# TensorE leaves out the products without use in the passages between stages

## The chip, the cores and the metric

The kernel runs on one core of one Trainium2 chip. The metric is the device time of one execution in microseconds (us). It is one program for a two-part transformer stack over 256 tokens of width 1024: an attention, RWKV and mixture-of-experts layer, followed by two layers of another block. Only passages of these two last layers are touched.

## The reference, cut to what matters

```python
def second_block(x, ...):
    for l in range(DEPTH_2):                      # DEPTH_2 = 2
        h = rms_norm_2(x, norm_mix_pre[l])
        proj = h @ w_in[l]                        # 1024 x 3072: 12 slices of 256
        ...                                       # convolution, two attentions, gated convolution
        mix = jnp.concatenate([y_conf, y_sb, y_ret, y_sc], axis=-1) @ w_out[l]
        x = x + rms_norm_2(mix, norm_mix_post[l])
        f = conv_ffn(rms_norm_2(x, norm_ffn_pre[l]), ffn_up[l], ffn_conv_w[l], ffn_down[l])
        x = x + rms_norm_2(f, norm_ffn_post[l])
    return x
```

Everything is float32. `rms_norm_2` divides each token by the root of its mean square and multiplies by a gain. Each layer has two places where a norm stands between two large products: x into the mixer (`w_in`) and x into the feed-forward part (`ffn_up`). A norm needs the whole row of a token, so the product ahead of it must be complete before the product behind it can start.

## The kernel before, in words

The kernel first runs the first block (front part, recurrence, experts) and then `layers_part` (L2628). Each engine there has one function with a fixed order of work: `layers_tensor` (TensorE, PE in the profile), `layers_scalar` (ACT), `layers_vector` (DVE), `layers_sync` (SP, which starts the loads). They meet in semaphores alone. `signalled` (L2708) waits for a count of a named signal, `free` (L2790) waits until a bank of PSUM has been read by its last user.

The stream x is kept with tokens on the partitions (`m.x_tok`), in two tiles t of 128 tokens. A product wants the channels on the partitions. `turn` (L2796) does the turning and the scaling by the norm in one step: for each tile t and each of the eight chunks c of 128 channels, one float32 product of the chunk with `scale_eye`, a 128x128 diagonal matrix of 1/root. It is called four times in all: `turn("turn_mix", 0)` at the head of each layer and `turn("turn_ffn", 2)` between mixer and feed-forward part of each layer. These are the four passages.

What runs in a passage, in the order of dependence:

- The last product before it (`tokens_product`, L2904, or the expert part's L2103) fills four banks: two halves of tile 0, then two halves of tile 1.
- ACT squares and sums each bank (L3044) and takes a root (L3049). DVE multiplies by the gain (L3182), scales and adds to x (L3188 or L3194).
- ACT squares the new x (L3020, or L3028 and L3032) and takes the second root (L3022 or L3036). DVE makes the reciprocal (L3169) and the diagonal (L3171), and signals "scaled" for this tile.
- TensorE waits for "scaled" (L2807) and turns the tile (L2810). ACT copies the banks to `x_hi` with the gain (L3061 or L3135), in a rounded format. DVE makes `x_lo`, what the rounding left (L3239 or L3366).
- The product behind the passage (`entry_product`, L2842) starts on the first chunk as soon as it is there. Weights are split likewise into `w_hi` (ACT, L3010) and `w_lo` (DVE, L3216), and each float32 product is made of three of the rounded format. After it come the long runs of `product` (L2868).

Between the last product before the passage and the turned tile, TensorE has nothing to do. In the kernel before, `turn` issues products there whose result nobody reads: a matrix of ones times a table, 512 columns wide, in float32, into a bank that is overwritten next. At `turn_mix` they stand ahead of tile 0 (L2801, two in the first layer and three in the second). At `turn_ffn` they stand between tile 0 and tile 1 (L2806, three in each layer), behind one more wait for a free bank.

Of the kernel before, what the change touches and what calls it, by code (L numbers as in the profile page):

```python
# [2627 lines left out]
def layers_part(nc, m, a, out, ctx):  # L2628
# [66 lines left out]
    def before(l, unit):  # L2695
        b, n = unit
        return l * USES[b] + n
# [10 lines left out]
    def signalled(eng, l, name, k):  # L2708
        eng.wait_ge(S[name], l * total[name] + k)
# [78 lines left out]
    def layers_tensor(pe):  # L2788
        for l in range(2):
            def free(name, k=0):  # L2790
                unit = UNIT[name, k]
                if before(l, unit) > 0:
                    pe.wait_ge(drained[unit[0]], before(l, unit))
                return unit[0]

            def turn(name, first):  # L2796

                banks = [free(name, n) for n in range(4)]

                for _ in range(0 if first > 0 else 3 if l > 0 else 2):  # L2800
                    pe.matmul(m.ps[:, banks[0], :], m.c("ones"), m.c("iota"), start=True, stop=True)  # L2801
                for t in range(TT):
                    if t > 0 and first > 0:
                        b = free("up_first")
                        for _ in range(3):
                            pe.matmul(m.ps[:, b, :], m.c("ones"), m.c("iota"), start=True, stop=True)  # L2806
                    signalled(pe, l, "scaled", first + t + 1)  # L2807
                    for c in range(KC):
                        cols = slice(c % 2 * SEQ + t * P, c % 2 * SEQ + (t + 1) * P)
                        mm = pe.matmul(m.ps[:, banks[c // 2], cols], m.x_tok[:, t, c * P:(c + 1) * P],  # L2810
                                       scale_eye[:, t, :], start=True, stop=True)
                        if t == TT - 1 and c % 2:
                            mm.then_inc(filled[banks[c // 2]], 1)
# [80 lines left out]
            def tokens_product(i, banks, x, chunk, first, last, tiles=range(TT)):  # L2894
# [15 lines left out]
                return mm  # L2910

            turn("turn_mix", 0)
            project("conf_a")
            project("conf_gate")
# [3 lines left out]
            b = free("vec")  # L2918
# [7 lines left out]
            for i, name in enumerate(("ret_q", "ret_k")):  # L2926
                await_drained(pe, l, name)
                b = free("swap", i)
# [3 lines left out]
            for h in range(4):  # L2932
                signalled(pe, l, "sb_masked", h + 1)
                b = free("tail", h)
# [16 lines left out]
            b = free("ret_mean")  # L2951
# [3 lines left out]
            b = free("ret_var")  # L2955
            pe.matmul(m.ps[:, b, :], m.c("pair_ones"), ret_sq[:, :, :], start=True, stop=True).then_inc(filled[b], 1)
            signalled(pe, l, "conf_done", 1)
            b = free("conf_mean")
# [4 lines left out]
            banks = [free("out", n) for n in range(4)]  # L2963
            for r, t in ((0, None), (1, None), (2, 0), (3, 0), (2, 1), (3, 1)):
# [6 lines left out]
                if r == 0:  # L2971
                    signalled(pe, l, "conf_squared", 1)
                    b = free("conf_var")
                    for c in range(2):
                        mm = pe.matmul(m.ps[:, b, 0:SEQ], m.c("ones"), conf_sq[:, c, :], start=(c == 0), stop=(c == 1))
                    mm.then_inc(filled[b], 1)
            turn("turn_ffn", 2)
            for q, (kind, n) in enumerate(FFN_ORDER):
                i = PIECE_FFN + q
# [6 lines left out]
                if n == 0:  # L2986
                    banks = [free("down", k) for k in range(4)]
# [526 lines left out]
```

## Time and profile before

| | |
|---|---|
| median of 3 runs | 1357.8 us (1356.83 to 1359.24) |
| the profiled execution's own time | 1356.83 us |
| its span, first to last instruction | 1355.0 us |
| PE busy | 1160.0 us (86%) |
| DVE busy | 737.7 us (54%) |
| ACT busy | 487.1 us (36%) |
| DMA queue q1 | 347.40 MB, 70.6% of 16 engines' time |
| mean granted TensorE clock | 0.939 |

The layers' part begins near 733 us. The four passages lie near 734, 850, 1042 and 1158 us. Before it, from some 320 to 730 us, the expert weights are loaded and the DMA engines are busy throughout; the granted clock of TensorE changes there between 1.00 (2.4 GHz) and 0.50 (1.2 GHz). In the rows below, a float32 product shows as two records of PE MATMUL and two of PEld LDWEIGHTS, and a row of a timeline merges neighbouring records of one line. The number in square brackets at the end is how long the engine had been idle before, and what released it. A row of the windows gives a stretch, its length, the busy time and instruction count of PE, PEld, DVE, ACT and POOL, then TensorE's granted clock, the share of the DMA engines and GB/s.

### The profile page before, as it was taken

How to read it: one execution, taken by the hardware profiler on the slowest of the kernel's cores; microseconds unless marked ns; L12 is line 12 of the kernel's file. 1: busy time of each engine (PE TensorE's matmuls, PEld its weight loads, DVE VectorE, ACT ScalarE, POOL GpSimd, SP SyncE). 2: the span in 40 equal slices, each digit the busy share in tenths (PEclk: the TensorE clock that was granted, in tenths of full speed). 3: DMA queues.
4: the chain of work that ended last, by engine and by line, in shares of the span. 5: the costliest groups of instructions: out<-in, count | busy, mean ns of one | idle time of the engine just before them, and what ended most of it. 6: DMA issues, size and time to landing. Idle time of an engine off the chain costs nothing.

```text
span 1355.0 us, 22776 instructions
## 1 busy us (share of the span) xinstructions
PE 1160.0 (86%) x9669; PEld 919.5 (68%) x9669; DVE 737.7 (54%) x1120; ACT 487.1 (36%) x657; POOL 2.6 (0%) x11
## 2 busy tenths in 40 slices
PE   7999989997657366564739999999999999999998
PEld 6998778973213121221314998999998998999997
DVE  5487655852101010010104898877777899877776
ACT  4543435330000000000004546644446556644444
POOL 0000000000000000000000000000000000000000
PEclk9999999998878697788869999999999999999999
DMA  8842225999999999999999646566655436566650
GB/s 270 281 149 63 65 80 210 342 405 416 426 427 424 428 427 424 429 426 427 426 419 361 212 149 179 160 201 186 187 156 179 156 127 181 172 189 187 187 156 31
DMA packets 180986, 349.52 MB, mean 258 GB/s; under 512 B 8140, under 2 KB 154737, under 8 KB 167954
## 3 DMA queue, kind: packets, MB, share of 16 engines
q1 hardware_dynamic: 180394, 347.40, 70.6%
q8 instruction: 79, 1.29, 0.4%
q10 hardware_dynamic: 488, 0.62, 0.2%
q14 instruction: 25, 0.20, 0.0%
HBM read 346.93 MB, written 3.43 MB: 259 GB/s over the span
## 4 chain that ended last, share of the span: by engine, by line
PE 66%; DMA 17%; DVE 3%; issue 2%; SPq 1%; ACT 1%; DVEq 1%; ACTq 0%
PE ps L2868 25%; PE ps L2904 12%; DMA expert_ring<-in_w_expert_up 7%; PE ps L2058 6%; DMA expert_top<-in_w_expert_up 4%; PE ps L2089 4%; DMA expert_early<-in_w_expert_up 2%; DMA expert_ring<-in_w_expert_gate 2%; PE ps L225 2%; PE ps L2046 2%; PE ps L1708 2%; PE ps L2103 2%; PE ps L254 2%; PE ps L2880 2%; PE ps L2842 2%
## 5 line engine op out<-in xcount | busy, mean ns | idle before, releaser
L3216 DVE TENSOR_TENSOR w_lo<-expert_early,w_hi 128x2048 fp32r<-128x2048 f32 x80 | 182.8, 2291 | 25.7 <-ACT w_hi L3010 22.9
L2058 PE MATMUL ps<-expert_ring,w_slot 128*32 128x512 f32 x640 | 113.6, 712 | 96.7 <-DMA expert_ring<-in_w_expert_gate 40.9
L2131 DVE TENSOR_TENSOR hT<-ps,hT 128x512 f32<-128x512 f32 x8 | 8.5, 1068 | 340.9 <-PE ps L2058 340.9
L3010 ACT ACTIVATE w_hi<-expert_early 128x2048 fp32r<-128x2048 f32 x80 | 153.0, 1918 | 56.5 <-PE ps L2904 34.1
L2058 PEld LDWEIGHTS ps<-expert_ring,w_slot 128*32 128x32 f32 x640 | 30.3, 129 | 159.5 <-issue 159.5
L2868 PE MATMUL ps<-x_hi,w_hi 128*128 128x256 f32 x960 | 134.2, 282 | 0.0
L2868 PE MATMUL ps<-x_hi,w_lo 128*128 128x256 f32 x960 | 134.1, 282 | 0.0
L2868 PE MATMUL ps<-x_lo,w_hi 128*128 128x256 f32 x960 | 132.3, 280 | 0.0
L2868 PEld LDWEIGHTS ps<-x_hi,w_hi 128*128 128x128 f32 x960 | 122.9, 188 | 3.8 <-issue 1.6
L2868 PEld LDWEIGHTS ps<-x_hi,w_lo 128*128 128x128 f32 x960 | 123.0, 190 | 0.0
L2868 PEld LDWEIGHTS ps<-x_lo,w_hi 128*128 128x128 f32 x960 | 121.0, 188 | 0.0
L3392 DVE SCALAR_TENSOR_TENSOR ff<-ps,ff_taps,ff 128x254 f32<-128x254 f32 (+1 forms) x176 | 76.8, 478 | 46.5 <-ACT ff L3150 43.3
L3150 ACT ACTIVATE ff<-ps,ff_taps 128x256 f32<-128x256 f32 x88 | 36.9, 471 | 118.2 <-PE ps L2868 117.4
L2058 PE MATMUL ps<-expert_early,w_slot 128*32 128x512 f32 x192 | 51.5, 698 | 23.3 <-DMA expert_ring<-in_w_expert_gate 12.4
L2110 ACT ACTIVATE hT<-ps 128x512 f32<-128x512 f32 x8 | 4.8, 597 | 171.4 <-PE ps L2068 171.4
L2058 PE MATMUL ps<-const,w_slot 128*32 128x512 f32 x48 | 31.8, 827 | 33.1 <-DMA expert_early<-in_w_expert_up 20.5
L2108 ACT ACTIVATE hT<-ps 128x512 f32<-128x512 f32 x8 | 4.8, 597 | 146.4 <-PE ps L2058 146.4
L2089 PE MATMUL ps<-expert_ring,hT 128*32 128x512 f32 x288 | 47.7, 633 | 8.6 <-issue 6.8
L3227 DVE SCALAR_TENSOR_TENSOR att_T<-conf_pad,vec,att_T 128x256 f32<-128x256 f32 x120 | 52.8, 481 | 3.8
L2058 PE MATMUL ps<-expert_top,w_slot 128*32 128x512 f32 x96 | 52.4, 709 | 0.0
L2904 PE MATMUL ps<-w_hi,hid_lo 128*128 128x512 f32 x176 | 48.9, 396 | 0.0
L2904 PE MATMUL ps<-w_lo,hid_hi 128*128 128x512 f32 x176 | 48.8, 395 | 0.0
(531 smaller groups left out, 2095.5 us busy)
## 6 DMA issues: line engine op xcount, KB each, us to landing
expert_ring<-in_w_expert_gate SPq DMA_DIRECT2D x22, 2048.0 KB, 29.4
expert_ring<-in_w_expert_up SPq DMA_DIRECT2D x18, 2048.0 KB, 29.3
expert_early<-in_ffn_up SPq DMA_DIRECT2D x36, 1024.0 KB, 6.0
expert_ring<-in_w_expert_down SPq DMA_DIRECT2D x14, 2048.0 KB, 29.8
w_slot<-in_w_in SPq DMA_DIRECT2D x26, 1024.0 KB, 5.5
expert_early<-in_w_in SPq DMA_DIRECT2D x20, 1024.0 KB, 5.5
expert_early<-in_ffn_down SPq DMA_DIRECT2D x18, 1024.0 KB, 4.9
expert_early<-in_w_expert_gate SPq DMA_DIRECT2D x6, 2048.0 KB, 26.9
```

What stands on the lines that cost most here:

```text
L225: mm = pe.matmul(m.ps[:, REC_BANKS + j, 0:SEQ], m.w_slots[gate_slot(g)][:, k, j * P:(j + 1) * P], m.hT[:, k, :], start=(k == 0), stop=(k = ...
L254: mm = pe.matmul(m.ps[:, REC_BANKS + j, 0:SEQ], pair[:, w, k, j * P:(j + 1) * P], x[:, k, :], start=(part == 0 and k == 0), stop=(part == ...
L1708: mm = pe.matmul(out, w[:, pair_of(i), col:col + P], x[y][:, x0 + k, :], start=(p == 0 and k == 0), stop=(p == 2 and k == n - 1))
L2058: mm = pe.matmul(m.ps[rows_of(e), b, :], x_quad[:, k, rows_of(e)], w[e][:, k, :], start=(k == 0), stop=(k == KC - 1))
L2089: mm = pe.matmul(m.ps[rows_of(e), DOWN + j, :], hidden_T[:, f, rows_of(e)], w[e][:, f, j * 512:(j + 1) * 512], start=(f == 0), stop=(f == ...
L2868: mm = pe.matmul(m.ps[:, b, j * SEQ:(j + 1) * SEQ], w[:, s, at(k, j):at(k, j) + P], x[:, k, :], start=(part == 0 and k == 0), stop=(part = ...
L2904: mm = pe.matmul(m.ps[:, banks[2 * t + c], :], xs[:, chunk + k, t * P:(t + 1) * P], w[:, s, k * D + c * 512:k * D + (c + 1) * 512], start= ...
L3010: act.activation(w_hi[:, half_slot(l, i), :], raw_slot(m, i), ACT.Copy).then_inc(S["w_hi"], 1)
L3150: ins = act.activation(ff[:, n % 2, j, :], m.ps[:, b, at:at + SEQ], ACT.Copy, scale=ff_taps[:, 2, j * FF + n:j * FF + n + 1])
L3216: dve.tensor_tensor(w_lo[:, s, :], raw_slot(m, i), w_hi[:, s, :].bitcast(F32), ALU.subtract).then_inc(S["w_lo"], 1)
L3227: dve.scalar_tensor_tensor(conf[:, c, :], src, tap, conf[:, c, :], ALU.mult, ALU.add)
L3392: ins = dve.scalar_tensor_tensor(x, m.ps[:, b, at:at + SEQ - back], ff_taps[:, 2 - back, j * FF + n:j * FF + n + 1], x, ALU.mult, ALU.add)
```

## The change

Both groups of unread products are taken out of `turn`, with the wait for a free bank that stood ahead of the second. Nothing else is changed.

```diff
                 banks = [free(name, n) for n in range(4)]
 
-                for _ in range(0 if first > 0 else 3 if l > 0 else 2):
-                    pe.matmul(m.ps[:, banks[0], :], m.c("ones"), m.c("iota"), start=True, stop=True)
                 for t in range(TT):
-                    if t > 0 and first > 0:
-                        b = free("up_first")
-                        for _ in range(3):
-                            pe.matmul(m.ps[:, b, :], m.c("ones"), m.c("iota"), start=True, stop=True)
                     signalled(pe, l, "scaled", first + t + 1)
                     for c in range(KC):
```

## Rows read from the trace of the kernel before

**Rows 1.** The page: busy time, and the chain that ended last, by engine.

```profile
PE 1160.0 (86%) x9669; PEld 919.5 (68%) x9669; DVE 737.7 (54%) x1120; ACT 487.1 (36%) x657; POOL 2.6 (0%) x11
...
PE 66%; DMA 17%; DVE 3%; issue 2%; SPq 1%; ACT 1%; DVEq 1%; ACTq 0%
```

**Rows 2.** Windows behind the passages: stretch, length, five engines' busy time, clock, DMA share, GB/s.

```profile
855.00:1041.00 186.00, 186.00 (x1322) 174.20 (x1321) 142.39 (x199) 97.37 (x117) 0.00 (x0) 1.00 0.64 190
1163.00:1348.00 185.00, 185.00 (x1316) 173.38 (x1316) 139.25 (x197) 93.15 (x113) 0.00 (x0) 1.00 0.53 157
```

**Rows 3.** Lines L2801 and L2806: records, ns min/median/max, first and last start.

```profile
L2801 PE MATMUL ps<-const x10: 590/591/593, 733.9 to 1043.1; 128*128 128x512 f32 x10
...
L2806 PE MATMUL ps<-const x12: 590/592/595, 849.5 to 1159.6; 128*128 128x512 f32 x12
```

**Rows 4.** Timeline of the passage at 850 us: start, length, engine, line.

```profile
847.76 1.95 PE L2810 MATMUL ps<-scale_eye,xT 128*128 128x128 f32 x16
...
852.96 2.05 PE L2810 MATMUL ps<-scale_eye,xT 128*128 128x128 f32 x16 [0.68 <-DVE scale_eye L3171]
...
854.76 0.48 PE L2842 MATMUL ps<-x_hi,w_hi 128*128 128x256 f32 x2
```

**Rows 5.** Timeline of the passage at 1158 us.

```profile
1155.62 1.95 PE L2810 MATMUL ps<-scale_eye,xT 128*128 128x128 f32 x16
...
1160.82 2.05 PE L2810 MATMUL ps<-scale_eye,xT 128*128 128x128 f32 x16 [0.68 <-DVE scale_eye L3171]
```

**Rows 6.** Timeline of the passage at 1042 us.

```profile
1040.47 0.62 PE L2904 MATMUL ps<-w_lo,hid_hi 128*128 128x512 f32 x2
...
1044.80 3.84 PE L2810 MATMUL ps<-scale_eye,xT 128*128 128x128 f32 x32 [1.13 <-DVE scale_eye L3171]
```

**Rows 7.** Timeline of the passage at 734 us, out of the expert part.

```profile
730.17 3.89 PE L2103 MATMUL ps<-w_slot,hT 128*128 128x512 f32 x8
...
736.17 3.84 PE L2810 MATMUL ps<-scale_eye,xT 128*128 128x128 f32 x32 [0.39 <-DVE scale_eye L3171]
...
740.78 0.50 PE L2842 MATMUL ps<-x_hi,w_lo 128*128 128x256 f32 x2 [0.54 <-DVE w_lo L3216]
```

**Rows 8.** Windows of the expert part: PE pauses, and what the clock did next.

```profile
369.56:372.61 3.05, 0.01 (x1) 0.04 (x2) 1.45 (x3) 0.00 (x0) 0.00 (x0) 1.00 1.01 430
...
372.92:376.33 3.41, 3.41 (x20) 1.08 (x16) 0.00 (x0) 0.00 (x0) 0.00 (x0) 0.50 1.03 437
...
546.67:549.42 2.75, 0.00 (x2) 0.03 (x1) 1.45 (x3) 0.00 (x0) 0.00 (x0) 1.00 1.00 423
...
550.42:553.83 3.41, 3.41 (x24) 1.10 (x18) 0.00 (x0) 0.00 (x0) 0.00 (x0) 0.50 1.03 432
666.12:668.78 2.66, 0.00 (x1) 0.03 (x1) 0.69 (x1) 0.00 (x0) 0.00 (x0) 1.00 1.01 431
...
669.88:673.29 3.41, 3.41 (x20) 1.09 (x16) 0.00 (x0) 0.00 (x0) 0.00 (x0) 0.50 0.99 418
```

**Rows 9.** Windows: a shorter pause with what follows, and work after a longer one.

```profile
607.63:609.88 2.25, 0.00 (x1) 0.04 (x2) 1.45 (x3) 0.00 (x0) 0.00 (x0) 1.00 1.01 430
609.88:616.00 6.12, 6.12 (x60) 2.30 (x64) 0.00 (x0) 0.00 (x0) 0.00 (x0) 1.00 1.01 426
...
333.36:338.79 5.43, 5.43 (x28) 1.57 (x32) 0.00 (x0) 0.00 (x0) 0.00 (x0) 0.50 0.98 416
```

**Rows 10.** Timeline of the expert part: work after a long pause, L2089 at either clock.

```profile
333.36 9.74 PE L2058 MATMUL ps<-expert_ring,w_slot 128*32 128x512 f32 x64 [6.50 <-DMA expert_ring<-in_w_expert_gate]
...
550.98 1.13 PE L2089 MATMUL ps<-expert_ring,hT 128*32 128x512 f32 x2
551.83 1.13 PE L2089 MATMUL ps<-expert_ring,hT 128*32 128x512 f32 x2
...
554.12 0.63 PE L2089 MATMUL ps<-expert_ring,hT 128*32 128x512 f32 x2
554.55 0.63 PE L2089 MATMUL ps<-expert_ring,hT 128*32 128x512 f32 x2
```

## The prediction

> **What bounds the kernel now.** I read the page first: TensorE is busy for 86% of the span and holds 66% of the chain that ended last [rows 1]. That is a mean over unlike parts, so I took windows of the layers' part. Between the second and third passage TensorE is busy for 186.00 of 186.00 us, behind the fourth for 185.00 of 185.00, all at a granted clock of 1.00 [rows 2], its 2.4 GHz level. DVE and ACT have room in the same windows (142 and 97 us of 186). So in the layers every microsecond that TensorE starts late or works slower reaches the end, and one saved on another engine is worth nothing. Only in the passages does TensorE wait: before tile 1 at 852.96 and at 1160.82, before tile 0 at 1044.80 and at 736.17, each time released by DVE's `scale_eye` [rows 4 to 7]. The reader is to see that the unread products lie in front of exactly these waits.
>
> **What goes, and its direct worth.** Line L2801 has 10 records and L2806 has 12 [rows 3]. A float32 product makes two, so 5 and 6 products go: 2 and 3 at the two `turn_mix`, 3 and 3 at the two `turn_ffn`. At 0.59 us a record, with overlap, that is at most 22 x 0.59 = 13 us of TensorE work. None of it is on the path: behind the last of them TensorE still stood idle for 0.39, 0.68, 1.13 and 0.68 us until the diagonal came [rows 4 to 7]. What sets the passage is ACT's and DVE's norm, which the change leaves alone. Taken out, the products make the pause longer and start nothing sooner: direct worth 0. The bound from the other side: a release could come earlier only if these products slow ACT or DVE, which no row shows; the nearest rows are the idle times themselves, and as a limit, not as a value, I take their sum, 2.9 us of gain. The wait for a free bank that goes with L2806 is worth 0 as well: `entry_product` waits for the same bank itself, and the products behind that wait ran as soon as tile 0 was turned. No queue is reordered: SP, POOL, ACT and DVE issue the same instructions.
>
> **What the pauses become.** From the end of the last useful record to the release:
>
> - 850 us: 847.76 + 1.95 = 849.71 to 852.96, 3.25 us [rows 4].
> - 1158 us: 1155.62 + 1.95 = 1157.57 to 1160.82, 3.25 us [rows 5].
> - 1042 us: 1040.47 + 0.62 = 1041.09 to 1044.80, 3.71 us [rows 6].
> - 734 us: 730.17 + 3.89 = 734.06 to 736.17, 2.11 us [rows 7].
>
> **What such a pause did in this trace.** The expert part has pauses of the same lengths, and the clock can be read behind them. After 3.05 us the clock was 0.50 (1.2 GHz) from 372.92 to 376.33, after 2.75 us from 550.42 to 553.83, after 2.66 us from 669.88 to 673.29 [rows 8]. In all three TensorE had already started again, 0.31, 1.00 and 1.10 us earlier, and was busy for the whole 3.41 us: the clock falls late and hits the work behind the pause. After 2.25 us it stayed at 1.00 [rows 9]. So three of my four pauses, at 3.25, 3.25 and 3.71, are longer than every pause after which it fell, and the fourth, at 2.11, is shorter than one after which it held. The Trainium skill has a rule that speaks against this change: "TensorE: Matmul & The Clock Gate", section "Why this matters for your kernels", says to leave no idle gap of more than about 3 us between bursts of matmuls if the clock is to stay up. By it the same three passages fall; the rows differ from it in that the clock fell after 2.66 and 2.75 us too, and by them the fourth passage is not safe by much.
>
> **The price of one fall.** With the clock at 0.50 one step of L2089 took 551.83 - 550.98 = 0.85 us, at 1.00 554.55 - 554.12 = 0.43 [rows 10]: half the speed. A stretch of 3.41 us at half speed does 1.7 us of work, so it costs 1.7 us if TensorE is bound by its own work throughout. It is: behind the release come 16 turning products (2.05 us), and L2842 starts at 854.76, before their end, with no wait [rows 4]. If the clock falls before the release, part of the stretch is spent waiting and costs less, down to 0; this the longer pauses make likelier. If the low clock lasts, it costs more: behind a pause of 6.50 us TensorE worked at 0.50 for 5.43 us from 333.36 on [rows 9, 10], which is 2.7 us lost. I take 1.5, near the three rows of like length.
>
> **The sum.** Three falls x 1.5 = +4.5 us. The passage at 734 us I take at 0: it probably holds, and if the clock falls there, the wait of 0.54 us for `w_lo` [rows 7], which does not depend on TensorE, absorbs a part, 1.7 - 0.5 = 1.2 us. Nothing gives these microseconds back: behind the passages TensorE has no idle time [rows 2] in which a delay could vanish, and no other engine's work has to move for it. The profiled execution's own time is 1356.83 us (span 1355.0 and 1.8 around it), so it would become 1361.3. It was the fastest of three; the median is 1357.8, 1.0 above it, and the same +4.5 makes that 1362.3 us. That is what I forecast.
>
> **The rivals.**
>
> - *The clock mostly holds.* The time stays, or at most one passage pays: +0 to +1.7, about 1358.5 us. For it: the 2.25 us pause that cost nothing, and that the work behind my pauses is of other shapes (L2810, L2842) than L2089's, so that the rows of the expert part are an analogy. Against: three pauses shorter than mine all cost a fall. It decides if two or more of the three long pauses pass at 1.00. Chance 0.17. This is the case that is not slower.
> - *The clock stays low longer.* The pause at 3.71 and those at 3.25 let it fall before the release, and it is not given back until work has gone on for longer, as at 333.36. Price 2.7 us per passage, 3 x 2.7 = 8.1, about 1366 us. For it: the 5.43 us row. Against: that pause was 6.50 us. Chance 0.11.
> - *The unread products were in the way.* They read SBUF and write PSUM while ACT and DVE run the norm, and their going lets the diagonal come sooner in all four passages. At most the 2.9 us above, 1355 us. For it speaks only that they overlap in time; no row shows ACT or DVE slowed. It would need each passage to save over 0.7 us and no fall. Chance 0.04.
>
> **How the numbers follow.** The forecast has 0.68. Its own range is 1360 to 1364.5: a fall may be worth 0.8 or 1.7, and the first passage may add 1.2. A difference within 0.2% (2.7 us) can't be told from no change here; the three runs of before themselves spread over 2.4 us. Slower by more than that: nearly all of the forecast's 0.68 and all of 0.11, less a little for two cheap falls, 0.75. Within: the 0.17, that little, and part of the last case, 0.21. Faster: 0.04. The range of 1358.6 to 1366.0 leaves out half of the first rival, the upper half of the second and the last.
>
> **What would show it.** Right: lines L2801 and L2806 are gone; the idle time before L2810 grows to 2.1 us (734), 3.25 (850, 1158) and 3.7 (1042), still released by DVE's `scale_eye`; the windows behind the releases show a granted clock of 0.50 for about 3.4 us at 850, 1042 and 1158; L2810's or L2842's records there take about twice as long; the passages end 1 to 2 us later each, and the long windows behind stay at 100% busy. The span from the release to the next passage grows by that and by nothing else. Wrong: a clock of 1.00 behind the long pauses with the time unchanged would refute the step from pause to fall; a fall with the time unchanged would refute that TensorE's own work sets the pace behind the release; a `scale_eye` that comes sooner against the end of the product before would bear out the last rival.

## The result, and the profile after

The changed kernel takes 1364.9 us (median of 8 executions, 1361.23 to 1366.85), the kernel before 1357.86 (median of 8). The ratio of the two is 1.0046 with an interval of 1.0036 to 1.0056: slower by 6.2 us, 4.9 to 7.6. (The medians themselves lie 7.0 us apart, the means 6.3.) It was forecast slower, at 1362.3 us and by 4.5.

The profiled execution took 1365.0 us of its own, with a span of 1363.2. First the page's line on the engines, then windows of the changed kernel's passages, the three long ones first and the one at 734 us in the last two rows: stretch, length, busy time and count of PE, PEld, DVE, ACT and POOL, granted clock, DMA share, GB/s.

```profile
PE 1157.7 (85%) x9647; PEld 922.5 (68%) x9647; DVE 738.2 (54%) x1120; ACT 487.7 (36%) x657; POOL 2.6 (0%) x11
```

```profile
851.04:853.22 2.18, 0.00 (x0) 0.00 (x0) 1.55 (x3) 1.39 (x4) 0.00 (x0) 1.00 0.00 0
853.22:854.29 1.07, 0.00 (x1) 0.01 (x1) 0.45 (x2) 0.35 (x2) 0.00 (x0) 0.50 0.00 0
854.29:860.04 5.75, 5.75 (x27) 5.75 (x28) 3.21 (x8) 4.45 (x9) 0.00 (x0) 0.50 0.01 1
860.04:862.00 1.96, 1.96 (x18) 1.96 (x18) 1.51 (x2) 1.96 (x2) 0.00 (x0) 1.00 0.00 0
1047.78:1048.91 1.13, 0.00 (x1) 0.03 (x1) 0.79 (x3) 0.79 (x2) 0.00 (x0) 0.50 0.00 0
1048.91:1054.61 5.70, 5.70 (x27) 5.70 (x28) 3.14 (x6) 1.71 (x6) 0.00 (x0) 0.50 0.36 106
1167.24:1167.51 0.27, 0.00 (x0) 0.00 (x0) 0.22 (x1) 0.00 (x0) 0.00 (x0) 0.51 0.00 0
1167.51:1170.66 3.15, 3.15 (x14) 3.15 (x15) 0.88 (x3) 1.85 (x5) 0.00 (x0) 0.50 0.00 0
735.44:737.55 2.11, 0.00 (x1) 0.00 (x1) 1.14 (x3) 1.58 (x5) 0.00 (x0) 1.00 1.13 352
737.55:748.00 10.45, 9.90 (x83) 9.71 (x84) 8.37 (x14) 8.81 (x13) 0.18 (x2) 1.00 0.89 297
```

In the last column but two the clock goes to 0.50 in each long pause, ahead of the release, and stays there while TensorE is 100% busy: for 5.75, 5.70 and 3.15 us behind the three releases. At 734 us it stays at 1.00, in the pause and behind the release at 737.55. In the kernel before it was 1.00 in all four places:

```profile
738.00:742.00 4.00, 3.46 (x31) 3.26 (x30) 3.43 (x4) 3.63 (x10) 0.00 (x0) 1.00 0.75 257
853.00:857.00 4.00, 4.00 (x35) 4.00 (x36) 2.15 (x5) 3.29 (x9) 0.00 (x0) 1.00 0.01 2
1045.00:1049.00 4.00, 4.00 (x37) 4.00 (x37) 3.07 (x6) 2.21 (x8) 0.00 (x0) 1.00 0.35 131
1161.00:1165.00 4.00, 4.00 (x36) 4.00 (x37) 2.28 (x6) 3.43 (x9) 0.00 (x0) 1.00 0.02 4
```

The timeline of the changed kernel shows what that does to the work, to be compared with [rows 4] and [rows 6]:

```profile
854.29 3.78 PE L2804 MATMUL ps<-scale_eye,xT 128*128 128x128 f32 x16 [3.25 <-DVE scale_eye L3165]
857.72 0.77 PE L2836 MATMUL ps<-x_hi,w_hi 128*128 128x256 f32 x2
...
1048.91 6.53 PE L2804 MATMUL ps<-scale_eye,xT 128*128 128x128 f32 x32 [3.80 <-DVE scale_eye L3165]
```

The line numbers are six lower than before, L2804 is L2810 and L2836 is L2842. Sixteen records take 3.78 us where they took 2.05, and 32 take 6.53 where they took 3.84. The pauses are 3.25 and 3.80 us long and end by the same releaser.

I measure a passage from its release to the first record of the long product behind it (L2868 before, L2862 after). These are differences of starts in the two timelines:

| passage | release, before | release, after | length, before | length, after | loss | time at 0.50 behind the release |
|---|---|---|---|---|---|---|
| 734 us | 736.17 | 737.55 | 10.18 | 10.14 | 0 | 0 |
| 850 us | 852.96 | 854.29 | 7.54 | 10.22 | 2.68 | 5.75 |
| 1042 us | 1044.80 | 1048.91 | 9.42 | 12.02 | 2.60 | 5.70 |
| 1158 us | 1160.82 | 1167.51 | 7.54 | 9.03 | 1.49 | 3.15 |

The three losses sum to 6.8 us. The spans differ by 1363.2 - 1355.0 = 8.2. Of the rest, 1.4 us are there before the first passage (736.17 against 737.55), in the part that the change doesn't touch; over all traces of this document that release lies anywhere between 734.97 and 738.48. The last 0.1 us is in the pause at 1042 us, which is 3.80 us long and not 3.71. The trace of before was of the fastest of its executions, which spread over 2.4 us. Between the long passages nothing is given back: TensorE is busy without a gap, as in [rows 2].

```profile
864.00:1044.00 180.00, 180.00 (x1274) 168.40 (x1273) 135.45 (x190) 91.30 (x108) 0.00 (x0) 1.00 0.65 194
1172.00:1355.00 183.00, 183.00 (x1304) 171.59 (x1304) 136.87 (x191) 90.81 (x107) 0.00 (x0) 1.00 0.54 159
```

### The profile page after: what moved, and what is told of

It reads as the page before. It is cut to its first block, busy times and chain, and to the rows that moved or that the text cites. A ratio compares the mean times of both kernels' runs of the same rounds, so it can differ in the third digit from the quotient of the medians.

```text
span 1363.2 us, 22732 instructions
## 1 busy us (share of the span) xinstructions
PE 1157.7 (85%) x9647; PEld 922.5 (68%) x9647; DVE 738.2 (54%) x1120; ACT 487.7 (36%) x657; POOL 2.6 (0%) x11
## 4 chain that ended last, share of the span: by engine, by line
PE 66%; DMA 16%; DVE 2%; issue 2%; SPq 1%; ACT 1%; DVEq 1%; ACTq 0%
PE ps L2862 25%; PE ps L2898 12%; DMA expert_ring<-in_w_expert_up 7%; PE ps L2058 6%; DMA expert_top<-in_w_expert_up 4%; PE ps L2089 4%; DMA expert_early<-in_w_expert_up 2%; DMA expert_ring<-in_w_expert_gate 2%; PE ps L225 2%; PE ps L2046 2%; PE ps L2836 2%; PE ps L1708 2%; PE ps L2103 2%; PE ps L254 2%; PE ps L2874 2%
## 5 line engine op out<-in xcount | busy, mean ns | idle before, releaser
L2862 PE MATMUL ps<-x_hi,w_hi 128*128 128x256 f32 x960 | 134.2, 282 | 0.0
L2862 PE MATMUL ps<-x_hi,w_lo 128*128 128x256 f32 x960 | 134.1, 282 | 0.0
L2862 PE MATMUL ps<-x_lo,w_hi 128*128 128x256 f32 x960 | 132.3, 280 | 0.0
L2862 PEld LDWEIGHTS ps<-x_hi,w_hi 128*128 128x128 f32 x960 | 122.9, 188 | 3.8 <-issue 1.6
L2862 PEld LDWEIGHTS ps<-x_hi,w_lo 128*128 128x128 f32 x960 | 123.0, 190 | 0.0
L2862 PEld LDWEIGHTS ps<-x_lo,w_hi 128*128 128x128 f32 x960 | 121.0, 188 | 0.0
L2089 PE MATMUL ps<-expert_ring,hT 128*32 128x512 f32 x288 | 46.0, 632 | 8.8 <-issue 7.4
```

The source lines that it names most:

```text
L2089: mm = pe.matmul(m.ps[rows_of(e), DOWN + j, :], hidden_T[:, f, rows_of(e)], w[e][:, f, j * 512:(j + 1) * 512], start=(f == 0), stop=(f == ...
L2862: mm = pe.matmul(m.ps[:, b, j * SEQ:(j + 1) * SEQ], w[:, s, at(k, j):at(k, j) + P], x[:, k, :], start=(part == 0 and k == 0), stop=(part = ...
```

## The experiments

Times are against runs of the kernel before on the same chip, in the same series (22 to 27 of them, medians 1358.22 to 1358.25 us). `after_again`, `after_third` and `full_joint` are the full change again; `after_third` is a single execution, taken for its trace. The theory: the unread products did nothing but hold TensorE's clock, and without them it falls in the pauses and slows the work behind. The rivals: the time comes from another place; the unread products also cost something of their own; what counts is the length of the idle time, or the mere fact that TensorE is occupied.

**Each half alone, and the whole again.** `ffn_none` and `ffn_joint` are one kernel, `mix_none` and `mix_joint` another, run in two series. The edits are against the kernel before.

```diff
# ffn_none, ffn_joint
-                    if t > 0 and first > 0:
-                        b = free("up_first")
-                        for _ in range(3):
-                            pe.matmul(m.ps[:, b, :], m.c("ones"), m.c("iota"), start=True, stop=True)
# mix_none, mix_joint
-                for _ in range(0 if first > 0 else 3 if l > 0 else 2):
-                    pe.matmul(m.ps[:, banks[0], :], m.c("ones"), m.c("iota"), start=True, stop=True)
```

> Only the unread products of the two turn_ffn passages are left out; those of turn_mix stay. Theory (a fall of the clock behind each long pause): pauses of 3.25 us there, clock at 0.50 behind both releases, +3 to +5 us (the changed kernel's trace lost about 2.7 and 1.5 us in these two), and the passages at 734 and 1042 us look as before. Rival (the time comes from somewhere else, e.g. the expert part, which ended 1.4 us later in the changed kernel's trace): within 1 us of before. Rival (falls come only together with the turn_mix pauses): clock 1.00 in both.

> Only the unread products of the two turn_mix passages are left out. Theory: the pause of 3.7 us at the head of layer 2 always lets the clock fall, the one of 2.1 us at the head of layer 1 in some executions: +2 to +3.5 us in all, and together with the kernel without turn_ffn's it makes up the +6.3 us of the full change (the parts add). Rival (the parts overlap or the cost is a shared one): the two parts sum to clearly more or less than 6.3 us.

> The full change once more, for a second trace and more times on the same chip as its parts. Theory: +5 to +7.5 us; the clock falls behind the three long pauses again, but the moment of each fall against the release differs from that of the first trace, and with it the loss of each passage (between 1 and 2.8 us). Rival (the fall sits at a fixed distance from the pause): the same losses of 2.7, 2.6 and 1.5 us again.

> The full change, for a third trace. Theory: each of the three long pauses shows one of three outcomes, no fall (loss 0), a fall near or behind the release (about 3.4 us at 0.50 behind it, loss about 1.55 us) or a fall some 0.7 us or more ahead of the release (5.7 to 6.2 us at 0.50 behind it, loss 2.6 to 2.9 us); in each, loss = 0.46 to 0.47 of the time at 0.50 behind the release. Rival (the loss doesn't go with the clock): a passage that falls outside this line by more than 0.3 us.

> The full change beside its two parts, on one chip in one series, to see whether the parts add: so far +2.8 and +2.0 against +6.3 and +6.6. Theory (each passage pays for itself): full = sum of the two parts within 1.2 us. Rival (a passage that falls makes the next more likely to): full exceeds the sum by 1.5 us or more once more.

> Only turn_ffn's unread products left out, for the sum. Theory: +2.5 to +4 us.

> Only turn_mix's unread products left out, for the sum. Theory: +2 to +3 us.

| left out | ratio, interval | times 1358.2 us |
|---|---|---|
| turn_ffn's, first series | 1.0021 (1.0012 to 1.0030) | +2.9 |
| turn_mix's, first series | 1.0015 (1.0006 to 1.0024) | +2.0 |
| both, first series | 1.0049 (1.0035 to 1.0063) | +6.7 |
| turn_ffn's, second series | 1.0023 (1.0012 to 1.0033) | +3.1 |
| turn_mix's, second series | 1.0016 (1.0007 to 1.0025) | +2.2 |
| both, second series | 1.0041 (1.0029 to 1.0054) | +5.6 |

In the second series the parts sum to 5.3 against 5.6, so nothing speaks against their adding. The first series' gap of 1.8 us did not come again, and the intervals overlap there too: it is within the scatter. `ffn_none` was expected at +3 to +5 us with a fall in both passages; it came out at +2.9, and its trace has a fall in one of the two.

Each trace gives the loss of each passage, measured as above. The full change has four traces, with twelve long pauses:

| trace (own time) | 734 us | 850 us | 1042 us | 1158 us |
|---|---|---|---|---|
| first (1365.0) | 0 | 2.68 | 2.60 | 1.49 |
| again (1362.69) | 0 | 0 | 1.51 | 2.91 |
| third (1360.1) | 0 | 0 | 1.51 | 2.90 |
| joint (1362.29) | 0.83 | 0 | 1.56 | 1.49 |
| only turn_ffn's, two traces | | 0; 1.67 | 0; 0 | 1.60; 1.58 |
| only turn_mix's, two traces | 0; 0 | 0; 0 | 1.52; 1.55 | 0; 0 |

So a long pause has three outcomes. The windows of the second trace (`after_again`) show all three, one after the other:

```profile
851.04:854.30 3.26, 0.00 (x2) 0.00 (x1) 2.01 (x5) 1.74 (x5) 0.00 (x0) 1.00 0.00 0
854.30:862.00 7.70, 7.70 (x66) 7.70 (x67) 5.53 (x9) 6.63 (x10) 0.00 (x0) 1.00 0.01 3
1046.25:1047.08 0.83, 0.83 (x7) 0.83 (x8) 0.00 (x0) 0.71 (x3) 0.00 (x0) 1.00 0.63 148
1047.08:1050.49 3.41, 3.41 (x18) 3.41 (x17) 3.02 (x5) 0.29 (x1) 0.00 (x0) 0.50 0.35 123
1163.13:1163.79 0.66, 0.00 (x1) 0.00 (x1) 0.45 (x2) 0.01 (x1) 0.00 (x0) 0.50 0.00 0
1163.79:1169.96 6.17, 6.17 (x29) 6.17 (x30) 3.51 (x8) 4.86 (x9) 0.00 (x0) 0.50 0.00 0
```

The pause of 3.26 us at 851 cost nothing at all. At 1046.25 TensorE was released, ran 0.83 us at full clock and then 3.41 us at half. At 1163.13 the clock fell 0.66 us ahead of the release and stayed down for 6.17 us of work. Over the traces the second outcome cost 1.49 to 1.67 us and the third 2.6 to 2.9; in each the loss is 0.44 to 0.49 of the time at 0.50 behind the release. Where TensorE's clock fell 0.62 to 1.13 us ahead of the release, the half-speed work lasted 5.7 to 6.2 us; where it fell 0.28 us ahead or later, 3.1 to 3.4 us. From its fall to its rise the clock was down for 6.83 us in every fall of the first kind and for 3.41 or 3.42 us in every one of the second. The dearer fall is thus one of double length, and its early start saves only what lies in the pause. No long passage lies off the line of loss against time at 0.50 by 0.3 us; the one at 734 us does, as shown below. The twelve pauses of the full change: 3 without loss, 5 of about 1.5, 4 of about 2.8, a mean of 1.55 us. `after_again` was expected to show a fall in all three, and one pause held; `after_third` was expected with losses of 0.46 to 0.47 per microsecond at 0.50, and gave 0.44 and 0.47.

Whether a pause brings a fall does go with its length. Over all traces where its products are left out, the pause of 3.80 us at 1042 brought one in 6 of 6, those of 3.25 us in 8 of 12, and that of 2.11 us at 734 in 1 of 7. But length is not all: with the same 3.25 us, the pause at 1158 brought a fall in 6 of 6 traces and the one at 850 in 2 of 6. No run tells what makes that difference.

**Only the two products at the head of layer 1.**

```diff
-                for _ in range(0 if first > 0 else 3 if l > 0 else 2):
+                for _ in range(0 if first > 0 else 3 if l > 0 else 0):
```

> Only the two unread products at the head of layer 1 are left out (pause 2.1 us). Theory: the clock holds in most executions, +0 to +0.6 us, and clock 1.00 at this passage in the trace. Rival (every pause pays): +1.2 us, clock 0.50 behind 737.

Ratio 0.9998 (0.9989 to 1.0007): no cost that can be measured, and clock 1.00 over 737.07 to 748.00. But the joint trace of the full change shows that this pause of 2.11 us isn't safe either:

```profile
737.63:737.84 0.21, 0.21 (x1) 0.21 (x2) 0.00 (x0) 0.21 (x1) 0.19 (x2) 1.00 1.22 429
737.84:741.25 3.41, 3.41 (x18) 3.41 (x17) 2.08 (x5) 1.91 (x2) 0.00 (x0) 0.50 0.88 316
```

The stretch of 3.41 us cost only 0.83 us here (11.01 against 10.18), where a stretch of that length cost 1.5 to 1.7 in the other passages. TensorE would have waited 0.54 us for `w_lo` anyway [rows 7], and this wait is gone in this trace; that accounts for most of the difference, and the remaining 0.1 to 0.3 us stay open.

**More, and fewer, unread products in the turn_ffn pauses.**

```diff
-                        for _ in range(3):
+                        for _ in range(6):        # ffn_six
+                        for _ in range(1):        # ffn_one
```

> Six unread products instead of three in each turn_ffn pause (nothing is left out). They take about 5.3 us, the pause is 3.25 us, so TensorE is still at them when the diagonal comes, by about 2 us. Theory (the cost of the change is the clock alone, and unread work costs only what reaches past the release): clock 1.00 in both passages, the release-to-end time of the passage unchanged at 7.7 us, and +2 x 2 = +4 us. DVE's diagonal comes at the same distance from the last product as before. Rival (unread work slows ACT and DVE): the diagonal comes later, more than +4 us.

> One unread product instead of three in each turn_ffn pause, which leaves 2.4 us of pause behind it. Theory (the share of the pause that TensorE works decides): between before and the kernel without them (+2.8 us), about +1, since pauses of 2.2 us held the clock and pauses of 2.7 us didn't. Rival (one product is enough): within 0.5 us of before. Rival (only a filled pause holds it): +2.5 us or more.

Six: 1.0029 (1.0017 to 1.0041), +3.9 us. This is the one slow kernel in whose trace the layers run at full clock throughout (1.00 over 734 to 1352). Its timeline at 850 us:

```profile
851.11 1.62 DVE L3194 SCALAR_TENSOR_TENSOR xT<-hT,norm_roots,xT 128x512 f32<-128x512 f32 x2
851.11 5.32 PE L2806 MATMUL ps<-const 128*128 128x512 f32 x12
...
854.18 0.28 DVE L3171 TENSOR_SCALAR scale_eye<-const,norm_roots 128x128 f32<-128x128 f32 x1
...
856.26 1.95 PE L2810 MATMUL ps<-scale_eye,xT 128*128 128x128 f32 x16
```

The diagonal is ready at 854.18 + 0.28 = 854.46, and TensorE comes to it at 856.26, 1.80 us late; in the kernel before it came 0.05 late. The passage at 1158 us gives 1.79 in the same way. Twice 1.75 is 3.5 of the 3.9 us. DVE's way from L3194 to the diagonal takes 854.18 - 851.11 = 3.07 us beside a TensorE that works throughout. In the kernel before, where the unread products fill 2.74 us of it, it takes 3.08, and in the changed kernel, where TensorE is idle all the time, 3.08 as well. First the two rows of before, then those of after:

```profile
849.54 1.62 DVE L3194 SCALAR_TENSOR_TENSOR xT<-hT,norm_roots,xT 128x512 f32<-128x512 f32 x2
852.62 0.29 DVE L3171 TENSOR_SCALAR scale_eye<-const,norm_roots 128x128 f32<-128x128 f32 x1
```

```profile
850.87 1.62 DVE L3188 SCALAR_TENSOR_TENSOR xT<-hT,norm_roots,xT 128x512 f32<-128x512 f32 x2
...
853.95 0.29 DVE L3165 TENSOR_SCALAR scale_eye<-const,norm_roots 128x128 f32<-128x128 f32 x1
```

The chain contains ACT's squares and root too. At 1042 us the way from the start of the last useful records to the start of DVE's diagonal is 1044.46 - 1040.47 = 3.99 us before and 1048.48 - 1044.48 = 4.00 after. So the unread products slow neither DVE nor ACT in these passages, and cost only where they reach past the release.

One: 1.0012 (1.0003 to 1.0021), +1.6 us, between three (0) and none (+2.9), as the theory had it. But the interval, +0.4 to +2.9 us, reaches into both rivals (within 0.5, and 2.5 or more), so the time alone doesn't decide. Its trace speaks against the rival that one product is enough, with a fall behind one of two equal pauses of 2.39 us:

```profile
852.62:855.01 2.39, 0.00 (x0) 0.00 (x0) 1.26 (x4) 1.53 (x5) 0.00 (x0) 1.00 0.00 0
855.01:863.00 7.99, 7.99 (x68) 7.99 (x69) 5.82 (x10) 6.82 (x11) 0.00 (x0) 1.00 0.01 3
1160.51:1162.90 2.39, 0.00 (x1) 0.00 (x1) 1.26 (x4) 1.52 (x5) 0.00 (x0) 1.00 0.00 0
1162.90:1163.84 0.94, 0.94 (x8) 0.94 (x9) 0.00 (x0) 0.19 (x1) 0.00 (x0) 1.00 0.00 0
1163.84:1167.25 3.41, 3.41 (x18) 3.41 (x18) 2.46 (x6) 3.41 (x9) 0.00 (x0) 0.50 0.02 5
```

**A small product in the middle of the pause.**

```diff
                     if t > 0 and first > 0:
                         b = free("up_first")
-                        for _ in range(3):
-                            pe.matmul(m.ps[:, b, :], m.c("ones"), m.c("iota"), start=True, stop=True)
+                        signalled(pe, l, "x_ready", first + t + 1)
+                        pe.matmul(m.ps[:, b, 0:P], m.c("ones"), m.c("iota")[:, 0:P], start=True, stop=True)
```

> As the kernel without turn_ffn's unread products, but one float32 product of 128 columns (about 0.2 us of TensorE work) stands in each of the two turn_ffn pauses, issued when DVE has finished the new x of tile 1, so that the pause of 3.25 us becomes two of about 1.5 us each. Theory A (what matters is how much TensorE works over the whole pause): no help, the clock falls as without it, +3 to +5 us over before. Theory B (what matters is the longest unbroken idle time): 1.5 us pauses never cost a fall in any trace here, so the clock stays at 1.00 and the time is that of before within 1 us.

```profile
852.57 0.46 PE L2806 MATMUL ps<-const 128*128 128x128 f32 x2 [1.63 <-DVEq L3196]
...
854.19 2.05 PE L2810 MATMUL ps<-scale_eye,xT 128*128 128x128 f32 x16 [1.16 <-DVE scale_eye L3171]
```

The pause is split into 1.63 and 1.16 us. The ratio is 1.0017 (1.0007 to 1.0027), +2.3 us, with executions up to 1365.04 us where before never passed 1359.78 in that series. That goes against the theory of the unbroken idle time, which forecast no more than 1 us; it lies below the +3 to +5 us of the other theory too, and is not told apart from no product at all (+2.9). The one trace shows clock 1.00 in both passages and a time of 1358.07 us, the lowest of its eleven, so the falls themselves were not seen here. The recorded mean clocks (below) speak for them; where they lie in the execution is inferred.

**The unread products in place, on one row of the array.**

```diff
-                    pe.matmul(m.ps[:, banks[0], :], m.c("ones"), m.c("iota"), start=True, stop=True)
+                    pe.matmul(m.ps[:, banks[0], :], m.c("ones")[0:1, :], m.c("iota")[0:1, :], start=True, stop=True)
-                            pe.matmul(m.ps[:, b, :], m.c("ones"), m.c("iota"), start=True, stop=True)
+                            pe.matmul(m.ps[:, b, :], m.c("ones")[0:1, :], m.c("iota")[0:1, :], start=True, stop=True)
```

> All eleven unread products stay at their places and lengths, but each uses one row of the array instead of 128 (one partition of ones and of the table). Theory A (the clock follows whether TensorE is occupied with matmuls): clock 1.00 in all four passages, time of before within 1 us. Theory B (it follows how much of the array works): clock 0.50 behind the long pauses as if they were empty, +5 to +7 us.

Ratio 1.0056 (1.0043 to 1.0069), +7.6 us: as slow as without them (+5.6 in the same series, 3.9 to 7.3), with overlapping intervals. The timeline and the windows of the passage at 850 us:

```profile
850.24 3.17 PE L2806 MATMUL ps<-const 1*128 1x512 f32 x6
853.57 3.78 PE L2810 MATMUL ps<-scale_eye,xT 128*128 128x128 f32 x16 [0.16 <-DVE scale_eye L3171]
```

```profile
850.24:852.63 2.39, 2.39 (x7) 1.03 (x6) 1.63 (x3) 1.44 (x4) 0.00 (x0) 1.00 0.00 0
852.63:853.41 0.78, 0.78 (x2) 0.00 (x0) 0.35 (x2) 0.29 (x1) 0.00 (x0) 0.50 0.00 0
853.57:859.46 5.89, 5.89 (x27) 5.89 (x28) 3.35 (x8) 4.58 (x9) 0.00 (x0) 0.50 0.00 1
```

The reader is to see that TensorE counts as busy for the whole stretch from 850.24 to 853.41, and that the clock falls at 852.63 in the midst of it. It fell in all four passages, which then lost 0.82, 2.77, 2.68 and 1.55 us, 7.8 in all. The idle time before the release was 0.16 us. So what holds the clock isn't that TensorE is occupied; the same products on all 128 rows held it, three of them (two at 734 us) or six, in every passage of every trace that has them, 23 passages in nine traces.

**The mean clock of every execution.** A trace shows one execution of each kernel, but the mean granted clock over the span is on record for all. A single value says little: the expert part has changes of its own, and executions of the kernel before alone run from 0.934 to 0.941. The means of the recorded values say more. They come in nearly the order of the times, with one exception:

| kernel | executions | mean of the clocks | times 1358.2 us |
|---|---|---|---|
| before, three series | 27, 22, 23 | 0.9367, 0.9367, 0.9366 | 0 |
| only layer 1's turn_mix products out | 11 | 0.936 | 0 |
| one product in turn_ffn's pauses | 11 | 0.935 | +1.6 |
| small product in turn_ffn's pauses | 11 | 0.935 | +2.3 |
| turn_ffn's out, two series | 11, 12 | 0.934, 0.934 | +2.9, +3.1 |
| turn_mix's out, two series | 11, 11 | 0.934, 0.934 | +2.0, +2.2 |
| full change, three series | 8, 5, 6 | 0.930, 0.930, 0.932 | +6.2, +6.7, +5.6 |
| one row of the array | 5 | 0.930 | +7.6 |
| six products in turn_ffn's pauses | 6 | 0.938 | +3.9 |

The six products are the exception, and they are the kernel whose loss isn't the clock's.

## Why the prediction was right, and where its sizes were off

- *What bounds the layers.* Right. A delay in a passage reached the end in full: 2.68 + 2.60 + 1.49 us lost, the end later by these, the 1.4 us from ahead of the first passage and 0.1 in a pause.
- *Direct worth of the products: 0.* Right. No release came sooner: the pauses became 3.25, 3.80, 3.25 and 2.11 us against the computed 3.25, 3.71, 3.25 and 2.11. The last rival (they are in the way of ACT and DVE) is refuted by 3.07 and 3.08 us for the same chain beside a working and an idle TensorE.
- *From pause to fall.* Right in kind, too certain: of the twelve long pauses of the full change nine cost a fall and three did not, where the forecast counted all. It says there that its three pauses are longer than every pause after which the clock fell in the trace of before; that holds for [rows 8], but not for the pause of 6.50 us in its own [rows 10]. The Trainium skill's rule of about 3 us ("TensorE: Matmul & The Clock Gate", section "Why this matters for your kernels") is no boundary here: pauses of 3.25 us held the clock four times in these traces, and pauses of 2.39 and 2.11 us let it fall once each.
- *The price of one fall.* This is the term that was mis-sized. I took 1.5 us for every fall, near the three rows of like length [rows 8], and gave the price of 2.7 us, from [rows 9], to a rival with a chance of 0.11. Both happen in the same kernel: 5 falls at 1.5 and 4 at 2.6 to 2.9. What separates them in the traces is whether the clock fell well ahead of the release. The prediction's term for that case was "part of the stretch is spent waiting and costs less, down to 0"; it is the dearer one, since the clock then stays down for 6.83 us and not for 3.41. The rival with 0.11, a fall ahead of the release and a clock that is given back later, had this mechanism right, at 2.7 us, but for all passages at once. That error (+) and the pauses without a fall (-) nearly cancel: the mean per long pause over the four traces is 1.55 us. That the 1.5 of the sum fits this mean is luck.
- *The sum.* +4.5 us against 4.9 in the mean of the four traces (18.65 us of the twelve pauses and 0.83 of one first passage, over four) and against 5.6 in the mean of all 20 executions of the full change (1364.0, before 1358.3). The first comparison's +6.2 is at the upper side of these, and its median of 1364.9 us lies just above the 1360 to 1364.5 that the prediction gave the forecast itself, though inside its whole range. What lies between 4.9 and 5.6 is within what four traces can tell, whose own times average 1362.5; no cause was looked for.
- *The passage at 734 us.* Taken at 0, with 1.2 us if it falls; it fell in one trace of four, at 0.83 us.

No kernel tried is faster than the kernel before. Its remaining idle times of 0.39 to 1.13 us show no fall in its trace, so there was nothing to gain from more unread work, and six products showed what too much costs.

## What to carry to other kernels

Before deleting work that nobody reads, or adding it, look at the granted clock behind the engine's pauses, not at the idle time in them: the price of a pause is paid by the work behind it. Padding costs nothing as long as it ends before the release, and it has to be work of the right kind: on all 128 rows of the array it held the clock, on one row it did not, and nothing between was tried. Where the outcome varies from execution to execution, one trace shows one draw; take several before giving the loss a size.

## What the runs showed of the hardware that was not expected

- Three products of 512 columns on one row of the array keep TensorE as busy in the profile as on 128 rows (a median of 588 ns a record against 592), yet the clock fell to 0.50 at 852.63 while they ran. The Trainium skill, in the same page's section "Terms", describes the gate as one that watches how busy the engine is. If that is the profile's busy time, this run contradicts it: the number of rows in use matters.
- The same pause in the same kernel gives 0, 1.5 or 2.8 us of loss from one execution to the next, and a single loss doesn't follow the length of the pause: 3.26 us cost nothing where 2.39 us cost 1.6. Only the share of pauses with a fall does (6 of 6 at 3.80 us, 8 of 12 at 3.25, 1 of 7 at 2.11).
- A fall well ahead of the release costs more than one behind it (2.6 to 2.9 us against 1.5 to 1.7), since the clock stays down for 6.83 us in place of 3.41.
- At half clock, the turning products and those of the rounded format together slow down by somewhat less than two: over all falls outside the first passage, 0.44 to 0.49 us were lost per microsecond at 0.50.
